# A 2-layer hybrid decoder step: the conformer convolution's products on GpSimd, three taps earlier, the fourth head's transposes in another bank

## What is computed

```python
def decoder_layer(x, lw, conv_a_buf, gla_state, conv_c_buf, fox_past):
    h = x + 0.5 * rms_norm(swiglu(rms_norm(x, f1_pre), f1_wg, f1_wu, f1_wd), f1_post)
    p_all = rms_norm(h, m_pre) @ w_in                    # D=1024 -> 3,088 columns
    ya, buf_a = conformer_conv(p_all[..., A], conv_a_buf, ...)   # 31 taps, depthwise
    yb, s_b   = gla_mixer(p_all[..., B], gla_state, ...)         # chunks of 64
    yc, buf_c = short_conv(p_all[..., C], conv_c_buf, c_cw)      # 3 taps
    yd        = fox_prompt / fox_decode(p_all[..., D], ...)      # 4 heads, softmax
    h = h + rms_norm(concat(ya, yb, yc, yd) @ w_out, m_post)
    h = h + 0.5 * rms_norm(swiglu(rms_norm(h, f2_pre), f2_wg, f2_wu, f2_wd), f2_post)

def conformer_conv(pa, buf, conv_w, conv_b, ln_g, ln_b):
    val, gate = split(pa, 2)
    a = val * sigmoid(gate)
    xpad = concatenate([buf, a], axis=1)                 # buf: 30 earlier rows
    y = causal_depthwise(xpad, conv_w) + conv_b          # 31 taps
    return silu(layer_norm(y, ln_g, ln_b)), xpad[:, -30:]
```

## Time and profile before

| | us |
|---|---|
| median of 3 runs | 1067.48 |
| lowest, highest | 1067.37, 1069.41 |
| the profiled execution's own time | 1067.81 |
| its span, first to last instruction | 1066.0 |

### The profile page before, as it was taken

The page is one execution under the profiler, slowest core; times in us unless marked ns, Lnnn a source line. Parts: engine busy times, 40 slices in busy tenths (PEclk is TensorE's granted clock), DMA queues, the critical chain, the costliest instruction groups (busy, mean ns, idle before and its releaser), DMA issues. The chain is left out here.

```text
span 1066.0 us, 24197 instructions
## 1 busy us (share of the span) xinstructions
PE 1052.3 (99%) x8978; PEld 1022.7 (96%) x8978; DVE 687.6 (64%) x1032; ACT 571.5 (54%) x970; POOL 278.4 (26%) x344
## 2 busy tenths in 40 slices
PE   8999999999999999999999999999999999999997
PEld 8999999998989999999999999999988999999997
DVE  5666644599977666654476666446999776666442
ACT  6544454576467644454464444546665765444542
POOL 4222220204505222220142222103054233222202
PEclk9999999999999999999999999999999999999999
DMA  7666577453735665556646656763536356665551
GB/s 277 216 180 186 175 223 235 127 160 92 226 100 182 199 192 179 180 168 184 185 135 199 179 177 186 234 200 118 174 102 213 109 176 216 179 188 175 174 182 49
DMA packets 62882, 187.42 MB, mean 176 GB/s; under 512 B 9162, under 2 KB 18514, under 8 KB 62674
## 3 DMA queue, kind: packets, MB, share of 16 engines
q1 hardware_dynamic: 62802, 186.31, 57.3%
HBM read 182.90 MB, written 3.38 MB: 175 GB/s over the span
## 5 line engine op out<-in xcount | busy, mean ns | idle before, releaser
L318 DVE TENSOR_TENSOR w_lo<-raw,w_hi 128x1024 fp32r<-128x1024 f32 (+1 forms) x316 | 412.3, 1310 | 321.7 <-ACT w_hi L308 321.6
L308 ACT ACTIVATE w_hi<-raw 128x1024 fp32r<-128x1024 f32 x336 | 344.9, 1032 | 238.5 <-PE ub L352 171.2
L350 PE MATMUL ub<-hg_hi,w_hi 128*128 128x264 f32 x976 | 281.2, 288 | 1.2 <-issue 1.2
L351 PE MATMUL ub<-hg_lo,w_hi 128*128 128x264 f32 x976 | 276.6, 283 | 0.0
L352 PE MATMUL ub<-hg_hi,w_lo 128*128 128x264 f32 x976 | 276.3, 283 | 0.0
L350 PE MATMUL ub<-act_hi,w_hi 128*128 128x264 f32 x704 | 200.5, 285 | 0.0
L352 PE MATMUL ub<-act_hi,w_lo 128*128 128x264 f32 x704 | 200.0, 284 | 0.0
L351 PE MATMUL ub<-act_lo,w_hi 128*128 128x264 f32 x704 | 199.1, 283 | 0.0
L350 PE MATMUL quad<-hg_hi,w_hi 128*128 128x264 f32 x696 | 198.6, 285 | 0.0
L351 PE MATMUL quad<-hg_lo,w_hi 128*128 128x264 f32 x696 | 197.2, 283 | 0.0
L352 PE MATMUL quad<-hg_hi,w_lo 128*128 128x264 f32 x696 | 197.1, 283 | 0.0
(11 more groups left out here) (259 smaller groups left out, 1285.3 us busy)
## 6 DMA issues: line engine op xcount, KB each, us to landing
raw<-in_w_gu SPq DMA_DIRECT2D x176, 512.0 KB, 4.0
raw<-in_w_dn SPq DMA_DIRECT2D x64, 512.0 KB, 3.9
raw<-in_w_in SPq DMA_DIRECT2D x44, 512.0 KB, 3.7
raw<-in_w_dn SPq DMA_DIRECT2D x32, 384.0 KB, 3.5
raw<-in_w_out SPq DMA_DIRECT2D x16, 512.0 KB, 3.7
pages<-in_cache_k SPq DMA_DIRECT2D x32, 128.0 KB, 3.4
pages<-in_cache_v SPq DMA_DIRECT2D x32, 128.0 KB, 3.1
con<-in_con SPq DMA_DIRECT2D x1, 1192.0 KB
```

The lines of the kernel that those rows point to most:

```text
L308: eng.activation(w_hi[:, slot, 0:w], raw[:, slot, 0:w], ACT.Copy).then_inc(*sig("hi_ready", reps))
L318: eng.tensor_tensor(w_lo[:, slot, 0:w], raw[:, slot, 0:w], w_hi[:, slot, 0:w].bitcast(F32), ALU.subtract)\
L350: eng.matmul(out, a_hi, x_hi[:, k0 + k, :], start=(first and k == 0), stop=False)
L351: eng.matmul(out, a_hi, x_lo[:, k0 + k, :], start=False, stop=False)
```

## The change

The products of the convolution leave VectorE. `a_pad` and `a_dec` are made by GpSimd in `conv_inputs`, behind `clear_pads` and ahead of all halves of `rest_halves`; the two products of the decoding rows are made by GpSimd in `conv_products`, ahead of the halves of unit 20. Three taps (0 to 2) move to step 11 on VectorE, where no PSUM bank is free yet; they accumulate in `ymix` in SBUF, and tap 3 reads from there and writes to the bank. The other taps are dealt out anew. Head 3's transposes go to bank `mb[2]` and wait for `d_dt` (the read of what stood there, VectorE's `d_tmp`) in place of `d_pt` = 1, and `d_all` moves on VectorE from step 23 to the end of the mixing of step 22.

```diff
--- before.py
+++ after.py
@@ -98,7 +98,8 @@
 LAST_TILES = 5
 FIRST_WARM = 11
 POOLED = tuple(range(14, 24))
-TAPS = {12: (0, 4), 13: (4, 10), 15: (10, 16), 16: (16, 22), 17: (22, 26), 18: (26, 28), 19: (28, 31)}
+TAPS = {11: (0, 3), 12: (3, 7), 13: (7, 11), 15: (11, 17), 16: (17, 23), 17: (23, 27), 18: (27, 30), 19: (30, 31)}
+EARLY_TAPS = 3
 
 INIT = {"split_done": RING, "unit_done": RING, "gu_read": 4, "y_scaled": 2, "silu_ready": 2, "act_ready": 2, "act_lo": 2,
         "hg_hi": 8, "h_sq": 8, "h_acc": 9, "hg_ready": 8, "y_acc": 1, "y_sum": 1, "stored": 3}
@@ -199,7 +200,7 @@
         NORM = mb[3][:, 0:NT]
         ROOT, SCALED = mb[1][:, 0:NT], (mb[2][:, 0:NT], ub[3][:, 0:NT])
         fox_bank = (mb[0], mb[1], ub[2], mb[2])
-        turned_bank = (mb[0], mb[1], ub[3], mb[0])
+        turned_bank = (mb[0], mb[1], ub[3], mb[2])
         taps_sum = ub[3]
 
         S = {n: ctx.enter_context(nc.semaphore(n)) for n in per}
@@ -657,7 +658,7 @@
             def fox_transposes(l, h):
                 after(l, d_pn=2 * h + 2)
                 if h == 3:
-                    after(l, d_pt=1)
+                    after(l, d_dt=1)
                 for i in range(3):
                     mm = pe.transpose(turned_bank[h][:, i * P:(i + 1) * P], sm[:, h, i * P:(i + 1) * P], ident)
                 mm.then_inc(*sig("d_pT"))
@@ -1185,14 +1186,17 @@
                 for t in range(first, last):
                     for c in range(2):
                         k = 2 * t + c
-                        y, x, w = taps_sum[:, c * TP:(c + 1) * TP], a_pad[:, c, t:t + TP], par[:, PAR["acw"] + c * TAPS_A + t:PAR["acw"] + c * TAPS_A + t + 1]
+                        x, w = a_pad[:, c, t:t + TP], par[:, PAR["acw"] + c * TAPS_A + t:PAR["acw"] + c * TAPS_A + t + 1]
+                        early, late = ymix[:, YA + c, 0:TP], taps_sum[:, c * TP:(c + 1) * TP]
                         if t == 0:
-                            after(l, b_msk=7)
-                            dve.tensor_scalar(y, x, w, par[:, PAR["acb"] + c:PAR["acb"] + c + 1], ALU.mult, ALU.add).then_inc(*sig("a_tap"))
+                            after(l, a_in=1)
+                            dve.tensor_scalar(early, x, w, par[:, PAR["acb"] + c:PAR["acb"] + c + 1], ALU.mult, ALU.add).then_inc(*sig("a_tap"))
                         else:
                             after(l, a_tap=k - 1)
-                            out = ymix[:, YA + c, 0:TP] if t == TAPS_A - 1 else y
-                            dve.scalar_tensor_tensor(out, x, w, y, ALU.mult, ALU.add).then_inc(*sig("a_tap"))
+                            if t == EARLY_TAPS:
+                                after(l, b_msk=7)
+                            out = early if t < EARLY_TAPS or t == TAPS_A - 1 else late
+                            dve.scalar_tensor_tensor(out, x, w, early if t <= EARLY_TAPS else late, ALU.mult, ALU.add).then_inc(*sig("a_tap"))
 
             def mix(l, n):
                 if n == 4:
@@ -1223,13 +1227,6 @@
                 if n == 10:
                     after(l, d_cf=1)
                     dve.tensor_scalar(cf[:, 0:TP], cf[:, 0:TP], -8.0, None, ALU.mult).then_inc(*sig("d_cf"))
-                if n == 11:
-
-                    after(l, a_sg=1, a_z=1, proj=10)
-                    dve.tensor_tensor(a_pad[:, :, TAPS_A - 1:], proj[:, AV:AV + 2, 0:TP], proj[:, AG:AG + 2, 0:TP], ALU.mult).then_inc(*sig("a_in"))
-                    after(l, past=PAST)
-                    dve.tensor_tensor(a_dec[:, :, :, TAPS_A - 1], proj[:, AV:AV + 2, TP:NT], proj[:, AG:AG + 2, TP:NT], ALU.mult)\
-                       .then_inc(*sig("a_in"))
                 if n == 13:
 
                     after(l, b_eb=1)
@@ -1270,11 +1267,6 @@
                     dve.tensor_scalar(sd[:, TP:TP + 1], mb[3][:, 320:321], DV ** -0.5, None, ALU.mult).then_inc(*sig("d_ds"))
                     after(l, d_ds=2)
                     dve.tensor_reduce(dstat[:, 1:2], sd[:, :], AX.X, ALU.max, negate=True).then_inc(*sig("d_dmx"))
-                    after(l, a_in=2)
-                    for c in range(2):
-                        dve.tensor_tensor(a_prod[:, c, :, :], a_dec[:, c, :, :],
-                                          par[:, PAR["acw"] + c * TAPS_A:PAR["acw"] + (c + 1) * TAPS_A].unsqueeze(1).to_broadcast([P, TD, TAPS_A]),
-                                          ALU.mult).then_inc(*sig("a_dp"))
                     after(l, a_dp=2)
                     dve.tensor_reduce(ymix[:, YA:YA + 2, TP:NT], a_prod[:, :, :, :], AX.X, ALU.add).then_inc(*sig("a_dr"))
                     after(l, a_dr=1)
@@ -1312,11 +1304,11 @@
                                       proj[:, DVV:DVV + 2, TP:NT], ALU.mult).then_inc(*sig("d_dt"))
                     short_conv(l, 1)
                     rest_mixed(l, YB)
-                if n == 23:
-                    short_gate(l, 0)
                     after(l, d_dpv=2)
                     dve.tensor_tensor(d_all[:, :, :].rearrange("p u (h v) -> p (u h) v", v=DV), mb[3][:, :].rearrange("p (a v) -> p a v", v=DV),
                                       const("own", 2 * H).unsqueeze(2).to_broadcast([P, 2 * H, DV]), ALU.mult).then_inc(*sig("d_dall"))
+                if n == 23:
+                    short_gate(l, 0)
                 if n == 24:
                     short_gate(l, 1)
                     after(l, a_rsd=2)
@@ -1487,6 +1479,22 @@
                 after(l, stored=0)
                 pool.memset(a_pad[:, :, 0:TAPS_A - 1], 0.0).then_inc(*sig("a_z"))
 
+            def conv_inputs(l):
+
+                after(l, a_sg=1, a_z=1, proj=10)
+                pool.tensor_tensor(a_pad[:, :, TAPS_A - 1:], proj[:, AV:AV + 2, 0:TP], proj[:, AG:AG + 2, 0:TP], ALU.mult).then_inc(*sig("a_in"))
+                after(l, past=PAST)
+                pool.tensor_tensor(a_dec[:, :, :, TAPS_A - 1], proj[:, AV:AV + 2, TP:NT], proj[:, AG:AG + 2, TP:NT], ALU.mult)\
+                    .then_inc(*sig("a_in"))
+
+            def conv_products(l):
+
+                after(l, a_in=2, b_o=1)
+                for c in range(2):
+                    pool.tensor_tensor(a_prod[:, c, :, :], a_dec[:, c, :, :],
+                                       par[:, PAR["acw"] + c * TAPS_A:PAR["acw"] + (c + 1) * TAPS_A].unsqueeze(1).to_broadcast([P, TD, TAPS_A]),
+                                       ALU.mult).then_inc(*sig("a_dp"))
+
             for t, name in ((qd[:, :], started), (pm[:, :], zeroed), (lfp[:, :], S["stored"]), (lfn[:, :], S["stored"])):
                 pool.memset(t, 0.0).then_inc(name, 1)
             for n, name in enumerate(("split_done", "unit_done", "gu_read", "y_scaled", "silu_ready", "act_ready", "act_lo", "y_acc", "y_sum", "stored")):
@@ -1499,7 +1507,10 @@
             for l in range(L):
                 feed_forward(l, 0)
                 clear_pads(l)
+                conv_inputs(l)
                 for n in POOLED:
+                    if n == 20:
+                        conv_products(l)
                     rest_halves(pool, l, n)
                 output_squares(l, 1)
                 input_squares(l, 1)
```

## The result

| | before | after |
|---|---|---|
| median of 7 runs each | 1067.93 | 1071.3 |
| lowest, highest | 1067.37, 1069.6 | 1070.87, 1071.96 |
| profiled execution, its span | 1067.81, 1066.0 | 1071.92, 1070.1 |

After / before is 1.0026, 95% interval 1.0017 to 1.0036: slower by 1.8 to 3.8 us. The forecast was 1072.0, or +4.5, so the direction and the range held, while the medians of the runs say about +3. The granted clock is 0.999 in both.

The account below looks back on a forecast made before the run. TensorE was taken as the bound, busy 1052.3 of 1066.0 us. Early loss 2 x 3.3 less late gain 2.1 gave +4.5 on 1067.81, 1072.3, or 1072.0 for the median; range 1066.5 to 1074.2.

Parts of the forecast that it names:

- early loss: Steps 10 to 12: GpSimd's product and the early taps delay VectorE; TensorE loses 2.6 to 3.4 us per layer, 3.3 taken.
- the product holds keys 6 by some 0.7: Step 10, VectorE: keys 6, ready at 244.30, begin only at 245.0 because GpSimd's a_pad runs (+0.7 us).
- the copy's row: Trace row of the parameters' copy, one input, SBUF to SBUF, 0.84 long, apparently held by GpSimd; basis for taking 3.3.
- Upper end: the scaling waits too, another half goes in between, and the evacuation starts at 249.65 (+3.1): Step 10, VectorE: worse case for unit 10's evacuation, 3.1 us late; TensorE's level 6 then 2.8 us late.
- w_lo over 2: Sign that the forecast is right: at step 10 the rest w_lo of unit 13 takes over 2 us on VectorE.
- the step on the early taps: Before evacuation 11: six taps cost 2.5 us alone, halves can slip in between; evacuation at 253.65 to 254.45 against 250.89.
- late gain: TensorE's waits at head 3 (0.7) and decode_gather (0.35) go: 2.1 us in both layers, lower bound 0.
- No wait of TensorE hangs on it besides those just counted, so I cost this at nothing: Moved decoding products and fewer taps leave VectorE some 4 us less behind by step 20; counted as no gain.
- GpSimd's product doesn't hold VectorE: Rival: keys 6 and w_lo go on as before, taps run free, evacuation 11 0.5 earlier; 1064.4; chance 0.18.
- Only w_lo is held, the taps aren't: Rival: evacuation 11 at about 252.2, level 6 alone holds TensorE, 1.3 us per layer; 1068.0; chance 0.10.
- Late gain lost: Rival: output projection starts 1 us earlier but waits for the short convolution's or heads' tiles; 1074.1; chance 0.03.
- Clock: Rival: TensorE standing still up to 2.8 us lowers the granted clock, adding 5.8 us; 1077.8; chance 0.02.

Follow-up runs that it names:

- the late part: Kernel before with only head 3's transposes in mb[2] behind d_dt and d_all at step 22; 1067.29 against 1068.83, ratio 0.9985.
- no early taps: The changed kernel with the table of taps and their code as in the kernel before; 1066.16, ratio 0.9977.
- products behind unit 14's halves: Changed kernel with the taps of the kernel before, and GpSimd making a_pad and a_dec two halves later; 1062.93, ratio 0.995.
- early-only kernel: The changed kernel with head 3's bank, its condition and d_all put back as before; 1073.25, ratio 1.0044.
- extra product: Kernel before plus one unused 128x512 product of constants on GpSimd, where the change puts a_pad; 1072.5, ratio 1.0032.

## Why the prediction was right, and where its sizes were off

**The early loss: right in mechanism and size (3.3 forecast, 3.15 measured), wrong in how it is put together.** The step that says the product holds keys 6 by some 0.7 measured 0.78. The price taken for the product from the nearest row, 1.29, was 1.28. The scaling was held under a half (forecast by the copy's row, measured 1.38 in place of 0.30). The step that failed is "Upper end: the scaling waits too, another half goes in between, and the evacuation starts at 249.65 (+3.1)". No half went in between: the second one, issued at 247.01, was overtaken by the rest of unit 13, issued at 247.12, and took 2.46 us in place of 1.29. So the sign "w_lo over 2" failed (it took 1.21), and level 6 was 1.6 late, near the lower end of 1.5, not the 2.8 of the upper end, near which the forecast was taken. What brought the total back near the forecast is the step on the early taps: "Two or three halves are still to come [...] and each can slip in between". Two did, and each held a `tensor_scalar` whose output is in SBUF, 1.30 in place of some 0.45. From evacuation 10 to 11 the forecast has 4.80 us at its upper end and 5.35 at its lower one; measured are 5.59. Evacuation 11 came 3.19 later (forecast 2.76 to 3.56), by another split of the same kind of waits: that the total came so near to 3.3 is in part luck, a loss put too high at step 10 and one put too low at step 11. Moving the scaling won only 0.2, so this hold wasn't the property of one instruction: the next one took it.

**The late gain: mis-sized.** The term was 1.05 per layer. By itself the late part gives 1.08, but as 1.38 and 0.07 won and 0.37 lost, the lower bound's mechanism in part. With the change's other parts it is 1.45, because evacuation 23 is no longer late. It is the table of the last taps that does this: with the decoding products moved but the old table the gain is 1.10 and 1.08 (no early taps, products behind unit 14's halves), and the new table adds 0.37 to the latter. The step "No wait of TensorE hangs on it besides those just counted, so I cost this at nothing" was therefore wrong by 0.37 (the change's 1.45 less 1.08); the same relief alone gave 0.5 in the early-only kernel. Two terms, 2 x (3.15 - 1.45), make +3.4 where the forecast had +4.5; the measured interval, 1.8 to 3.8, holds the first and not the second. The forecast time of 1072.0 lay 0.7 above the measured median.

**The extra 0.9 us.** Not foreseen, and no part of the change. The spans of the two profiled executions differ by +4.1, near the +3.4 with this 1.0 on top; taken at face value it would have made the forecast look better than it was.

**The rivals.** "GpSimd's product doesn't hold VectorE" fell with keys 6 at 1.47 and, by itself, with the extra product's 1.0032. "Only w_lo is held, the taps aren't" fell in both halves: w_lo went through at 1.21 and the first two taps were held; its remark that taps were seen only with PSUM was the right worry, since in the bank of `taps_sum` two of them took 1.00 beside a half (products behind unit 14's halves), as in the earlier trace rows. "Late gain lost": not lost, though 0.37 of it is when made alone. "Clock": TensorE stood still for 1.56 and 1.35 us in the first layer, not for the 2.8 of the rival, and the granted clock stayed at the upper level, 0.999. The kernel before had already stood still for 1.4 ahead of L793, at the same clock.

## What to carry to other kernels

Before moving an elementwise product from VectorE to GpSimd, lay both timelines over each other and ask what VectorE does with two SBUF inputs, or from SBUF to SBUF, in the 1.3 us in which the product would run: here the same product lost 0.28 us per layer at head 0 or won 1.35, by standing two instructions earlier or later in GpSimd's program. Draw work ahead only if somebody waits for its result: the taps drawn ahead of an evacuation that TensorE needs delayed it by their own length and by what held them there, and cost 2.87 us per layer at head 0. And the gaps between the starts of TensorE's instructions, not the idle times in brackets, give what a wait costs.

## What the runs showed of the hardware that was not expected

- Issue order did not always decide. In the change a half issued 0.11 us before the rest of unit 13 (247.01 against 247.12) was overtaken by it and took 2.46 us in place of 1.29. The same pair came out the same way in two more kernels: issued 247.26 against 247.37 without early taps, 247.38 against 247.49 with the extra product. In the kernel before, the half issued at 249.39 went ahead of `a_dec`, issued at 249.71, which is the order of issue. The section of the Trainium skill cited above has it that issue order decides who blocks; the second case agrees, the first differs from it by 0.11 us. My reading is that the request has to stand for some time before the other engine's instruction ends; it may also be that GpSimd's recorded start lies ahead of its request. No run separates these.
- A `tensor_scalar` from SBUF to SBUF is held completely by a reading GpSimd instruction, though it has one tensor input: 97x256 takes 0.30 alone and 1.38 held, the taps of 128x256 took 1.37 and 1.38 (free ones of this shape on other tiles 0.35). The taps with their output in PSUM take 0.55 and weren't held: two took 1.00 beside the half from 250.29. The section of the Trainium skill cited above lists `tensor_scalar` among those that can lock the port pair; the row agrees.
- A `scalar_tensor_tensor` with both tensors in SBUF is held as well. The early ones met no half, but the later start of everything moved the state updates (L1244, 128x256) beside the halves from 262.86: the six of both layers take 0.48 to 1.37 us, median 0.82, where the same six take 0.48 to 0.49 in the kernel before. The three of the first layer take 2.73 together in place of 1.52. It costs TensorE nothing that shows: its wait at `decode_scores` stays 0.86.
- GpSimd's product of 16 elements per partition takes 0.23 alone, 0.68 when keys 6 hold it.
